# Forgetting loop with values of n-2, turns of n-1 and scores of n in one place; band and convolution with scores and values of neighbouring pairs together

## The chip, the cores and the metric

One core of a Trainium2 chip runs the whole program in one launch. The metric is the device time of an execution in microseconds (us): 1598.29 is the median of three runs of the kernel before, which lie between 1597.94 and 1598.76. The engines go by their names: TensorE (PE) multiplies, VectorE (DVE) and ScalarE (ACT) work element by element, GpSimd (POOL) and SyncE (SP) mostly start transfers. Each engine runs its own queue of instructions in order, and semaphores join the queues.

## The reference, cut

Two transformer blocks for 256 tokens with 1024 features, in float32. Three of their attention layers lie where the change is made:

```python
# first block, second layer: chunked ("band") attention, 12 heads of 64, beside 4 heads over a memory
s = jnp.einsum('bqhd,bkhd->bhqk', qc, kc) * scale + bias
p = jax.nn.softmax(jnp.where(valid, s, -jnp.inf), axis=-1)
o = jnp.einsum('bhqk,bkhd->bqhd', p, vc)
...
# second block, first layer: a convolution over 31 tokens with a layer norm and silu, beside
# sliding-window attention ("swa"), 8 heads of 64, 2 heads of keys and values
a = u * jax.nn.sigmoid(gate)
y = lax.conv_general_dilated(a, w, padding=[(CONV_K - 1, 0)], feature_group_count=CONV_CH) + b
yf = (y - mu) * lax.rsqrt(var + EPS) * ln_g + ln_b
...
# second block, second layer: forgetting attention ("fox"), 16 heads of 64
c = jnp.cumsum(log_sigmoid(zf + b_f))
sc = jnp.einsum("bhqd,bhkd->bhqk", qs, kh) / math.sqrt(dh) + cs[..., :, None] - c[..., None, :]
p = jax.nn.softmax(jnp.where(tpos >= key_pos, sc, NEG), axis=-1)
o = jnp.einsum("bhqk,bhkd->bhqd", p, vh)
return o.reshape(b, s, h * dh) @ w_out
```

Each layer ends in a product with w_out, and swiglu or convolutional feed-forward layers (FFN) stand between them.

## The kernel before

The order of every engine is written out by hand, one block for each: sync (from L571), gpsimd (L728), scalar (L856), vector (L1471) and tensor (L2213). No planner moves anything.

Weights stream through 520 slots of 128 x 1024 floats, in a ring of ten. SyncE loads a slot; `splits(t)` on ScalarE casts it to the high part w_hi (L870, 1 cast a slot); `splits(t)` on VectorE subtracts to get the low part w_lo (L1488). TensorE multiplies both with the activations, which are split in the same way, so a float32 product is three matmuls (`mm`, L2215 and L2216). Both engines work through the slots in order, and so each `splits` in their queues stands before all later work of that engine.

A projection of two heads (a part, `part(name, bank, i)`) has two halves i of 24 matmuls each and one slot each half; VectorE takes it out of its PSUM bank when both are done (`take_part`, L2007, and `take_pair` for the forgetting layer). An output chunk (`out_chunk`, called as `band_out(i, b)`, `swa_out(i, b)`, `fox_out(i, b)`) is six matmuls for features i and output half b.

Attention works on pairs of heads. A pair n goes through: `scores` on TensorE (L2462; L2456 is the decay row of the forgetting layer), `scores` on VectorE (masked sums with their maxima, L1696 and L1709), `exps` on ScalarE (L1059), `probs` on VectorE (reciprocal L1718 and the normalising product L1722), `turns` on TensorE (transposes, L2475), `pt_copy` on ScalarE (L1071), `values` on TensorE (L2485 and L2488), and `o_hi` on ScalarE (L1077) and `o_lo` on VectorE (L1728), which put the result by in two parts. All of a pair's PSUM lies in one of four places, handed out by WAYS (L223); `scores` waits until the pair that had the place before has been put by (`before[g]`). Probabilities alternate between two buffers.

In the forgetting layer TensorE (L2990 to L3027) runs over m = 1 to 3 with the parts of pair m, and between their halves come the scores of pairs 2m - 2 and 2m - 1, their turns and the values of the pair before. Pairs 6 and 7 come between output chunks. The loops of ScalarE (L1447 to L1464) and VectorE (L2187 to L2207) follow m in the same way. The slots of the parts are 430 + 4m + 2 part + i, the output's slots are 446 to 453, and the next FFN starts at 454. `splits(t + 8)` inside the loops belongs to a slot that TensorE reads four half parts later.

In the band layer (ScalarE from L1279, VectorE from L2009, TensorE from L2756) pairs 0 and 1 are those of the memory, and pairs 2 to 7 follow; projections of queries, keys and values (`band_part`, `project("VB", b)`) and output chunks lie between the steps. In the convolution layer (ScalarE from L1372, VectorE from L2087, TensorE from L2899) `stack`, `conv` and `turn_u` stand between the steps of four pairs. `conv(2)` and `conv(3)` read the turned u, which GpSimd's queue writes to DRAM and reads back stacked (L832 to L849). `mean` and `variance` belong to the layer norm.

The loop of the forgetting layer on TensorE, and those on the other two:

```python
for m in range(1, 4):                          # TensorE, L2990
    fox_part(m, 0, 0)
    if m > 1: values("fox", 2 * m - 3)
    fox_scores(2 * m - 2)
    fox_part(m, 0, 1)
    fox_scores(2 * m - 1)
    fox_part(m, 1, 0)
    turns("fox", 2 * m - 2)
    fox_part(m, 1, 1)
    ...
```

Of the kernel before, what the change touches and what calls it, by code (L numbers as in the profile page):

```python
# [14 lines left out]
NCH = D // P  # L15
SEQ = 256
NTB = SEQ // P
# [218 lines left out]
def build(nc, x, mem, norm_mix_g, norm_ffn_g, a_w_in, a_gate_b, a_conv_w, a_conv_b, a_head_g, a_w_out,  # L236
# [5 lines left out]
    with ctx:  # L242
# [614 lines left out]
        def _(act):  # L857
# [449 lines left out]
            exps("band", 4)  # L1307
            splits(133)
            pt_copy("band", 3)
            o_hi("band", 2)  # L1310
            splits(134)
            take_v("VB", 0, HALF, SEQ)
            pt_copy("band", 4)
            o_hi("band", 3)
# [11 lines left out]
            splits(139)  # L1326
            o_hi("band", 6)
            pt_copy("band", 7)
            splits(140)
            o_hi("band", 7)  # L1330
# [66 lines left out]
            take_gate(1, 1)  # L1397
            exps("swa", 3)
            take_turned_u(2)
            pt_copy("swa", 2)  # L1400
            splits(286)
            conv_out(0)
            splits(288)
            conv_out(1)
            o_hi("swa", 2)
            pt_copy("swa", 3)
            splits(289)
            o_hi("swa", 3)
# [38 lines left out]
            for m in range(4):  # L1447
                t = fox_slots(m, 0)
                splits(t + 8)
                if m == 3:  # L1450
                    o_hi("fox", 5)
                exps("fox", 2 * m)
                if m in (1, 2):
                    o_hi("fox", 2 * m - 1)
                splits(t + 9)
                exps("fox", 2 * m + 1)
                pt_copy("fox", 2 * m)
                splits(t + (11 if m == 3 else 10))
                pt_copy("fox", 2 * m + 1)
                o_hi("fox", 2 * m)  # L1460
# [11 lines left out]
        def _(dve):  # L1472
# [566 lines left out]
            splits(129)  # L2039
            take_part("K1", bank[4], qk[:, 8:10, :])  # L2040
            scores("band", 3)
            probs("band", 2)
            splits(131)
            scores("band", 4)
            probs("band", 3)
            splits(132)
            take_part("K2", bank[5], qk[:, 10:12, :])
            o_lo("band", 2)
            probs("band", 4)
            splits(134)  # L2050
            o_lo("band", 3)
# [10 lines left out]
            probs("band", 7)  # L2062
            o_lo("band", 6)
            splits(139)
# [47 lines left out]
            scores("swa", 3)  # L2112
            probs("swa", 2)
            splits(285)
            take_u(1, 1)
            take_turned_u(3)
# [70 lines left out]
            for m in range(4):  # L2187
                t = fox_slots(m, 0)
                if m:
                    o_lo("fox", 2 * m - 2)  # L2190
                splits(t + 8)
                scores("fox", 2 * m)
                if m:
                    o_lo("fox", 2 * m - 1)
                if m < 3:
                    take_pair(m + 1, 0)
                probs("fox", 2 * m)
                scores("fox", 2 * m + 1)
                splits(t + 9)
                probs("fox", 2 * m + 1)  # L2200
                splits(t + (11 if m == 3 else 10))
                if m < 3:
                    take_pair(m + 1, 1)
            o_lo("fox", 6)
            splits(454)
# [8 lines left out]
        def _(pe):  # L2214
# [565 lines left out]
            scores("band", 2)  # L2780
            values("band", 1)
            band_part("K1", bank[4], 1)
            scores("band", 3)
# [5 lines left out]
            turns("band", 3)  # L2789
            values("band", 2)  # L2790
            project("VB", 0)
            turns("band", 4)
            values("band", 3)
# [19 lines left out]
            values("band", 6)  # L2813
            turns("band", 7)
            band_out(3, 1)
            band_out(5, 0)
            band_out(4, 1)
            values("band", 7)
            band_out(6, 0)
            band_out(7, 0)  # L2820
            band_out(5, 1)
# [96 lines left out]
            project("GU1", 1, {3: [lambda: scores("swa", 3)]})  # L2918
# [6 lines left out]
            values("swa", 2)  # L2925
            turns("swa", 3)
            mean(0)
            mean(1)
            values("swa", 3)
            pe.wait_ge(u_taken[2], 1)  # L2930
            pe.wait_ge(u_taken[3], 1)
            swa_out(0, 1, 0)
# [119 lines left out]
```

## Time and profile before

| what | value |
|---|---|
| median of three runs | 1598.29 us |
| the profiled execution | 1599.74 us |
| its span in the trace | 1598.0 us |
| mean granted clock of TensorE, as a share of 2.4 GHz | 0.999 |
| TensorE busy with matmuls | 1587.4 us, 99% |
| its weight loads | 1354.9 us, 85% |
| VectorE busy | 1092.2 us, 68% |
| ScalarE busy | 919.5 us, 58% |
| GpSimd busy | 56.2 us, 4% |

Busy times are shares of the span. Matmuls are pipelined and the trace models their ends, so neighbouring ones overlap in the rows; start times are the recorded ones. In a timeline a row is a run of equal instructions: when it starts, how long it lasts, engine, line, operation, output and inputs, shapes and count; brackets at its end give the idle time of the engine before it and who ended that. The chain of waits follows the work that ended last back through whatever released it.

### The profile page before, as it was taken

Reading aid. Unit: us, or ns where it says so; the run is one execution under the profiler, and the core shown is the slowest. Engines: PE = TensorE matmul, PEld = TensorE weight load, DVE = VectorE, ACT = ScalarE, POOL = GpSimd, SP = SyncE. Lnnn points to the kernel's source line nnn. Section 1 sums busy time; section 2 is a strip of 40 time slices with the busy share of each in tenths; the row PEclk is TensorE's granted clock in tenths of the full one; section 3 lists DMA queues with packets and bytes.
Section 4 is the critical chain, followed back from the end, with each engine's and each line's share of the span. In section 5 each row is a group of like instructions: output and inputs, shape, how many; then the busy total and the mean of one; then the engine's idle time right before and its main releaser. Section 6 shows DMA issues by size and latency. Waiting matters only on the chain.

```text
span 1598.0 us, 23594 instructions
## 1 busy us (share of the span) xinstructions
PE 1587.4 (99%) x9256; PEld 1354.9 (85%) x9256; DVE 1092.2 (68%) x1759; ACT 919.5 (58%) x1555; POOL 56.2 (4%) x96
## 2 busy tenths in 40 slices
PE   9999999999999999999999999999999999999998
PEld 7898888889788888888887788888888889888887
DVE  5986867778677768656677466567565667775665
ACT  6766645567655546545476664447444484664544
POOL 4000000000030000000002100000000000000000
PEclk9999999999999999999999999999999999999999
DMA  8545675554355565566655555655666564356662
GB/s 299 146 146 189 217 238 192 186 174 144 118 193 190 175 199 179 188 197 189 191 159 161 143 191 186 196 185 171 210 185 188 181 200 146 119 184 199 184 189 75
DMA packets 212401, 287.67 MB, mean 180 GB/s; under 512 B 11100, under 2 KB 180382, under 8 KB 212292
## 3 DMA queue, kind: packets, MB, share of 16 engines
q1 hardware_dynamic: 208676, 280.00, 55.3%
q0 software_dynamic: 3616, 6.17, 1.4%
q8 instruction: 74, 1.21, 0.3%
q14 instruction: 35, 0.29, 0.1%
HBM read 284.47 MB, written 3.87 MB: 180 GB/s over the span
## 4 chain that ended last, share of the span: by engine, by line
PE 97%; DMA 1%; ACT 1%; issue 0%; SPq 0%; DVE 0%; POOL 0%; DVEq 0%; ACTq 0%
PE two L2216 91%; PE two L2293 1%; PE two L2462 1%; PE two L2475 1%; PE two L2485 1%; PE two L2870 0%; DMA vals<-u_dram 0%; PE two L2279 0%; PE two L2488 0%; DMA raw<-in_mem_w_kv 0%; PE two L2626 0%; DMA raw<-in_ffn_w_up 0%; DMA u_dram<-aux 0%; PE two L2456 0%; PE two L2844 0%
## 5 line engine op out<-in xcount | busy, mean ns | idle before, releaser
L2216 PE MATMUL two<-act_parts,w_hi 128*128 128x512 f32 (+1 forms) x2784 | 801.7, 353 | 0.0
L1488 DVE TENSOR_TENSOR w_lo<-raw,w_hi 128x1024 fp32r<-128x1024 f32 (+1 forms) x520 | 613.1, 1221 | 105.8 <-ACT w_hi L870 105.6
L2216 PE MATMUL two<-act_parts,w_lo 128*128 128x256 f32 x2256 | 635.0, 281 | 0.0
L2216 PEld LDWEIGHTS two<-act_parts,w_hi 128*128 128x128 f32 x2784 | 487.0, 188 | 81.1 <-issue 5.3
L870 ACT CAST w_hi<-raw 128x1024 fp32r<-128x1024 f32 (+1 forms) x522 | 516.6, 1046 | 5.5 <-DMA raw<-in_ffn_w_up 5.0
L2216 PEld LDWEIGHTS two<-act_parts,w_lo 128*128 128x128 f32 x2256 | 425.5, 189 | 2.1
L2216 PE MATMUL two<-w_hi,act_parts 128*128 128x512 f32 (+2 forms) x832 | 248.6, 378 | 1.5 <-ACT w_hi L870 1.2
L999 ACT COPY p_sb<-two 128x512 f32<-128x512 f32 x108 | 62.4, 578 | 247.1 <-PE two L2216 247.1
L2216 PE MATMUL two<-w_hi,hid_even 128*128 128x512 f32 x576 | 187.8, 393 | 0.0
L2216 PEld LDWEIGHTS two<-w_hi,act_parts 128*128 128x128 f32 x832 | 150.2, 188 | 33.4 <-issue 3.6
L1616 DVE TENSOR_TENSOR pt_sb<-two,p_sb 128x512 f32<-128x512 f32 x54 | 37.3, 691 | 198.4 <-ACT p_sb L999 198.4
L2216 PE MATMUL two<-w_hi,hid_odd 128*128 128x512 f32 x496 | 162.4, 394 | 0.0
L2216 PE MATMUL two<-w_lo,act_parts 128*128 128x512 f32 (+2 forms) x416 | 152.7, 372 | 0.0
L2216 PEld LDWEIGHTS two<-w_hi,hid_even 128*128 128x128 f32 x576 | 108.1, 188 | 25.3
L2216 PE MATMUL two<-w_lo,hid_even 128*128 128x512 f32 x288 | 113.5, 394 | 0.0
L2216 PEld LDWEIGHTS two<-w_hi,hid_odd 128*128 128x128 f32 x496 | 93.1, 188 | 22.1 <-issue 0.3
L2216 PE MATMUL two<-w_lo,hid_odd 128*128 128x512 f32 x248 | 97.7, 394 | 0.0
L2216 PEld LDWEIGHTS two<-w_lo,act_parts 128*128 128x128 f32 x416 | 78.1, 188 | 13.6 <-DVE w_lo L1488 0.4
L1020 ACT ACTIVATE p_sb<-pt_sb 128x512 f32<-128x512 f32 x60 | 38.0, 633 | 77.6 <-DVE pt_sb L1639 60.3
L920 ACT ACTIVATE act_parts<-two,par 128x128 fp32r<-128x128 f32 x160 | 44.5, 378 | 37.9 <-PE two L2293 37.8
L2216 PEld LDWEIGHTS two<-w_lo,hid_even 128*128 128x128 f32 x288 | 54.0, 188 | 11.5
L1505 DVE SCALAR_TENSOR_TENSOR act_parts<-two,par,act_parts 128x128 fp32r<-128x128 f32 x160 | 43.7, 343 | 24.2 <-ACT act_parts L920 24.2
(318 smaller groups left out, 1198.8 us busy)
## 6 DMA issues: line engine op xcount, KB each, us to landing
raw<-in_ffn_w_up SPq DMA_DIRECT2D x160, 512.0 KB, 3.9
raw<-in_ffn_w_down SPq DMA_DIRECT2D x132, 512.0 KB, 3.5
raw<-in_ffn_w_gate SPq DMA_DIRECT2D x80, 512.0 KB, 3.7
raw<-in_a_w_in SPq DMA_DIRECT2D x24, 512.0 KB, 4.3
raw<-in_fox_w_in SPq DMA_DIRECT2D x20, 512.0 KB, 3.8
raw<-in_ffn_w_up SPq DMA_DIRECT2D x32, 256.0 KB, 3.5
raw<-in_w_kv SPq DMA_DIRECT2D x12, 512.0 KB, 3.8
raw<-in_a_w_out SPq DMA_DIRECT2D x8, 512.0 KB, 3.8
```

Of the source, the lines that this page charges most:

```text
L870: nc.scalar.copy(w_hi[:, t % RING, k * n:(k + 1) * n], raw[:, t % RING, k * n:(k + 1) * n]).then_inc(hi_done, 1)
L920: nc.scalar.activation(act_part(0, c, b), x_turned(idx, b, c), ACT.Copy, scale=cols(col, c)).then_inc(ah, 1)
L999: nc.scalar.copy(half_sb[part], wide_half(part, 1)).then_inc(ff_half[part], 1)
L1020: nc.scalar.activation(gate_act, gate_cv_all if conv else gate_all, ACT.Silu).then_inc(ff_act, 1)
L1488: nc.vector.tensor_tensor(w_lo[:, r, 0:n], raw[:, r, 0:n], w_hi[:, r, 0:n], ALU.subtract).then_inc(lo_done, 1)
L1505: nc.vector.scalar_tensor_tensor(out=act_part(1, c, b), in0=x_turned(idx, b, c), scalar=cols(col, c), in1=act_part(0, c, b), op0=ALU.mult, ...
L1616: nc.vector.tensor_tensor(dst, wide_half(part, 0), half_sb[part], ALU.add).then_inc(ff_sum[part], 1)
L2216: return nc.tensor.matmul(dst, a, w, start=start, stop=stop, skip_group_check=True)
L2293: ins = nc.tensor.transpose(x_turned(idx, b, c), x_tok[:, b, c * P:(c + 1) * P], ident[:, :])
L2462: ins = nc.tensor.matmul(dst[half][:, lo:hi], q[:, b * P:(b + 1) * P], k[:, 0:hi - lo], start=kind != "fox", stop=True, skip_group_check=True)
L2475: ins = nc.tensor.transpose(place[g][:, half * 512 + dst:half * 512 + dst + P], p_sb[:, g % 2, half * 512 + src:half * 512 + src + P], ide ...
L2485: nc.tensor.matmul(place[g][DH * half:DH * (half + 1), 0:SEQ], head_v(kind, h0 + half, 0), pt_sb[:, g % 2, half * 512:half * 512 + SEQ], s ...
```

## The change

Only the order of calls changes, on three engines; no instruction is added or taken away, and nothing changes on SyncE's and GpSimd's queues.

- Forgetting layer: TensorE's loop has, after every second half part, one place where values of pair n - 2, turns of n - 1 and scores of n stand directly behind each other (`fox_stages(n)`). Before, scores 2m - 2 and 2m - 1 stood on either side of a half part and turns and values in places of their own. The last pairs follow the same pattern among the output chunks. ScalarE's loop becomes one over n with two casts, `o_hi(n - 2)`, `pt_copy(n - 1)` and `exps(n)` in each turn; VectorE's has two splits, `o_lo(n - 2)`, `scores(n)`, `take_pair` and `probs(n)`.
- Band layer: scores 3 go directly behind scores 2, values 2 in front of values 3 and behind the first half of the values' projection, values 6 directly in front of values 7. ScalarE's and VectorE's calls are moved to suit.
- Convolution layer: scores 3 come out of the gate and u projection and stand directly before the convolution; values 2 join values 3; output chunk (1, 0) goes ahead of conv(2); the chunks (1, 1) and (2, 0) stand around the variance. ScalarE copies turned probabilities 2 ahead of the turned u, VectorE takes scores 3 later.

The diff, with one line of context on either side of each place (`...` where lines are left out):

```diff
@@ -1305,13 +1305,13 @@
 exps("band", 4)
+pt_copy("band", 3)
 splits(133)
-pt_copy("band", 3)
-o_hi("band", 2)
 splits(134)
 take_v("VB", 0, HALF, SEQ)
+o_hi("band", 2)
+o_hi("band", 3)
 pt_copy("band", 4)
-o_hi("band", 3)
 splits(135)
@@ -1323,10 +1323,9 @@
 exps("band", 7)
-splits(139)
-o_hi("band", 6)
 pt_copy("band", 7)
 splits(140)
+o_hi("band", 6)
 o_hi("band", 7)
@@ -1395,17 +1394,18 @@
 take_gate(1, 1)
+pt_copy("swa", 2)
+take_turned_u(2)
 exps("swa", 3)
-take_turned_u(2)
-pt_copy("swa", 2)
 splits(286)
 conv_out(0)
+splits(287)
+conv_out(1)
+pt_copy("swa", 3)
 splits(288)
-conv_out(1)
 o_hi("swa", 2)
-pt_copy("swa", 3)
+o_hi("swa", 3)
 splits(289)
-o_hi("swa", 3)
 fetch_table(ACT.Sqrt)
@@ -1444,20 +1444,27 @@
 splits(435)
-for m in range(4):
-    t = fox_slots(m, 0)
+for n in range(6):
+    t = fox_slots(0, 0) + 2 * n
+    splits(t + 7)
+    if n >= 2:
+        o_hi("fox", n - 2)
+    if n >= 1:
+        pt_copy("fox", n - 1)
+    exps("fox", n)
     splits(t + 8)
-    if m == 3:
-        o_hi("fox", 5)
-    exps("fox", 2 * m)
-    if m in (1, 2):
-        o_hi("fox", 2 * m - 1)
-    splits(t + 9)
-    exps("fox", 2 * m + 1)
-    pt_copy("fox", 2 * m)
-    splits(t + (11 if m == 3 else 10))
-    pt_copy("fox", 2 * m + 1)
-    o_hi("fox", 2 * m)
+o_hi("fox", 4)
+pt_copy("fox", 5)
+splits(449)
+exps("fox", 6)
+splits(451)
+o_hi("fox", 5)
+pt_copy("fox", 6)
+splits(452)
+exps("fox", 7)
+splits(454)
+o_hi("fox", 6)
+pt_copy("fox", 7)
 splits(455)
@@ -2037,17 +2044,17 @@
 splits(129)
+probs("band", 2)
 take_part("K1", bank[4], qk[:, 8:10, :])
 scores("band", 3)
-probs("band", 2)
 splits(131)
+probs("band", 3)
 scores("band", 4)
-probs("band", 3)
 splits(132)
 take_part("K2", bank[5], qk[:, 10:12, :])
-o_lo("band", 2)
 probs("band", 4)
 splits(134)
+o_lo("band", 2)
 o_lo("band", 3)
@@ -2060,8 +2067,8 @@
 probs("band", 7)
+splits(139)
 o_lo("band", 6)
-splits(139)
 o_lo("band", 7)
@@ -2109,10 +2116,10 @@
 splits(284)
-scores("swa", 3)
 probs("swa", 2)
 splits(285)
 take_u(1, 1)
+scores("swa", 3)
 take_turned_u(3)
@@ -2184,25 +2191,27 @@
 take_pair(0, 1)
-for m in range(4):
-    t = fox_slots(m, 0)
-    if m:
-        o_lo("fox", 2 * m - 2)
+for n in range(6):
+    t = fox_slots(0, 0) + 2 * n
+    splits(t + 7)
+    if n >= 2:
+        o_lo("fox", n - 2)
+    scores("fox", n)
     splits(t + 8)
-    scores("fox", 2 * m)
-    if m:
-        o_lo("fox", 2 * m - 1)
-    if m < 3:
-        take_pair(m + 1, 0)
-    probs("fox", 2 * m)
-    scores("fox", 2 * m + 1)
-    splits(t + 9)
-    probs("fox", 2 * m + 1)
-    splits(t + (11 if m == 3 else 10))
-    if m < 3:
-        take_pair(m + 1, 1)
+    take_pair(n // 2 + 1, n % 2)
+    probs("fox", n)
+o_lo("fox", 4)
+scores("fox", 6)
+splits(450)
+probs("fox", 6)
+splits(451)
+o_lo("fox", 5)
+scores("fox", 7)
+splits(452)
+probs("fox", 7)
+splits(454)
 o_lo("fox", 6)
-splits(454)
+splits(455)
 o_lo("fox", 7)
@@ -2778,19 +2787,19 @@
 scores("band", 2)
+scores("band", 3)
 values("band", 1)
 band_part("K1", bank[4], 1)
-scores("band", 3)
 band_part("K2", bank[5], 0)
 turns("band", 2)
 pe.wait_ge(fp_taken, PI["K1"] + 1)
 scores("band", 4)
 band_part("K2", bank[5], 1)
 turns("band", 3)
+project("VB", 0)
 values("band", 2)
-project("VB", 0)
+values("band", 3)
 turns("band", 4)
-values("band", 3)
 pe.wait_ge(fp_taken, PI["K2"] + 1)
@@ -2810,15 +2819,15 @@
 band_out(2, 1)
-values("band", 6)
 turns("band", 7)
 band_out(3, 1)
 band_out(5, 0)
+values("band", 6)
+values("band", 7)
 band_out(4, 1)
-values("band", 7)
+band_out(5, 1)
 band_out(6, 0)
 band_out(7, 0)
-band_out(5, 1)
 out_end("band", band_ready, 1)
@@ -2915,33 +2924,36 @@
 stack(1)
-project("GU1", 1, {3: [lambda: scores("swa", 3)]})
+project("GU1", 1)
+scores("swa", 3)
 conv(0, 0, QUADS // 2)
 turns("swa", 2)
 turn_u(2)
 turn_u(3)
 conv(0, QUADS // 2)
 conv(1)
-values("swa", 2)
 turns("swa", 3)
 mean(0)
 mean(1)
+values("swa", 2)
 values("swa", 3)
 pe.wait_ge(u_taken[2], 1)
 pe.wait_ge(u_taken[3], 1)
 swa_out(0, 1, 0)
 pe.wait_ge(h_olo, PAIR0["swa"] + 4)
 swa_out(0, 0, 0)
+swa_out(1, 0)
 conv(2)
 conv(3)
 mean(2)
 mean(3)
+swa_out(1, 1)
+out_chunk("swa", swa_ready, 2, 0, (0,))
+variance()
+out_chunk("swa", swa_ready, 2, 0, (1,))
+swa_out(2, 1)
 for b in range(NTB):
-    swa_out(1, b)
-variance()
-for i in range(2, 4):
-    for b in range(NTB):
-        swa_out(i, b)
+    swa_out(3, b)
 for b in range(NTB):
@@ -2987,43 +2999,40 @@
 pe.wait_ge(gates_m, 2)
+def fox_stages(n):
+    if n >= 2:
+        values("fox", n - 2)
+    if n >= 1:
+        turns("fox", n - 1)
+    if n < 8:
+        fox_scores(n)
+
 for m in range(1, 4):
     fox_part(m, 0, 0)
-    if m > 1:
-        values("fox", 2 * m - 3)
-    fox_scores(2 * m - 2)
+    fox_stages(2 * m - 2)
     fox_part(m, 0, 1)
-    fox_scores(2 * m - 1)
     fox_part(m, 1, 0)
-    turns("fox", 2 * m - 2)
+    fox_stages(2 * m - 1)
     fox_part(m, 1, 1)
-    if m < 3:
-        turns("fox", 2 * m - 1)
-        values("fox", 2 * m - 2)
-values("fox", 4)
-turns("fox", 5)
 pe.wait_ge(h_olo, PAIR0["fox"] + 4)
 fox_out(0, 0)
+fox_stages(6)
 fox_out(1, 0)
-fox_scores(6)
-values("fox", 5)
 pe.wait_ge(h_olo, PAIR0["fox"] + 5)
 fox_out(0, 1)
 fox_out(1, 1)
-fox_scores(7)
-for b in range(NTB):
-    fox_out(2, b)
-turns("fox", 6)
-for b in range(NTB):
-    fox_out(3, b)
-turns("fox", 7)
-values("fox", 6)
+fox_out(2, 0)
+fox_stages(7)
+fox_out(2, 1)
+fox_out(3, 0)
+fox_out(3, 1)
 fox_out(4, 0)
+fox_stages(8)
+fox_out(4, 1)
 values("fox", 7)
 fox_out(5, 0)
 out_end("fox", pair_ready("fox", 0), 0)
-for i in range(4, NCH - 2):
-    fox_out(i, 1)
+fox_out(5, 1)
 out_end("fox", pair_ready("fox", 0), 1)
```

## Rows read from the trace of the kernel before

**Rows 1.** The page's fourth part: the chain that ended last, by engine.
```profile
PE 97%; DMA 1%; ACT 1%; issue 0%; SPq 0%; DVE 0%; POOL 0%; DVEq 0%; ACTq 0%
```

**Rows 2.** Windows: us, busy PE, PEld, DVE, ACT, POOL (instructions), clock, DMA share, GB/s.
```profile
1329.00:1405.00 76.00, 76.00 (x555) 64.23 (x554) 53.64 (x153) 45.81 (x110) 0.00 (x0) 1.00 0.40 122
880.00:893.00 13.00, 11.62 (x152) 7.06 (x151) 3.92 (x4) 5.73 (x9) 2.78 (x5) 1.00 0.65 128
```

**Rows 3.** Timeline, TensorE, forgetting stage: first row of each group of matmuls.
```profile
1347.18 0.50 PE L2216 MATMUL two<-act_parts,w_hi 128*128 128x256 f32 x2
...
1350.22 0.44 PE L2456 MATMUL two<-rowf,pick 64*128 64x384 f32 x2
...
1351.25 0.50 PE L2216 MATMUL two<-act_parts,w_hi 128*128 128x256 f32 x2
...
1354.21 0.82 PE L2475 MATMUL two<-ident,p_sb 128*128 128x128 f32 x6
1354.79 0.48 PE L2216 MATMUL two<-act_parts,w_hi 128*128 128x256 f32 x2
...
1357.72 0.82 PE L2475 MATMUL two<-ident,p_sb 128*128 128x128 f32 x6
1358.46 0.65 PE L2485 MATMUL two<-pt_sb,vals 128*64 128x256 f32 x4
...
1359.27 0.50 PE L2216 MATMUL two<-act_parts,w_hi 128*128 128x256 f32 x2
```

**Rows 4.** Timeline, TensorE, forgetting stage: turns that stand behind values.
```profile
1375.60 0.87 PE L2475 MATMUL two<-ident,p_sb 128*128 128x128 f32 x6
1376.23 0.48 PE L2216 MATMUL two<-w_hi,fox_parts 128*128 128x512 f32 x1
```

**Rows 5.** Chain of waits in order of time: start us, us, what.
```profile
398.17 0.76 PE two L2475 x6
398.93 0.86 PE two L2462 x8
...
402.83 0.80 PE two L2475 x6
...
843.62 1.51 PE two L2462 x16
...
1357.88 0.66 PE two L2475 x6
...
1388.82 2.79 PE two L2216 x12
```

**Rows 6.** Timeline, VectorE and ScalarE, softmax of a forgetting pair.
```profile
1347.31 0.29 DVE L1696 CUSTOM_DVE_ANT_0 aux<-two,causal 128x128 f32<-128x128 f32 x1 [1.17 <-PE two L2462]
...
1348.54 0.17 DVE L1709 TENSOR_SCALAR small<-small 128x4 f32<-128x4 f32 x1
...
1350.42 0.19 ACT L1059 ACTIVATION_READ_ACCUMULATOR p_sb<-aux,small 128x1 f32 x1
...
1350.77 1.05 ACT L870 CAST w_hi<-raw 128x1024 fp32r<-128x1024 f32 x1
...
1350.90 0.42 DVE L1728 TENSOR_TENSOR fox_parts<-two,fox_parts 128x256 fp32r<-128x256 f32 x1 [2.19 <-ACT fox_parts L1077]
1351.24 0.68 DVE L2007 TENSOR_TENSOR qk<-two,rstd 128x512 f32<-128x512 f32 x1
...
1352.05 1.01 DVE L1722 TENSOR_SCALAR p_sb<-p_sb,small 128x128 f32<-128x128 f32 x4
...
1354.28 1.22 DVE L1488 TENSOR_TENSOR w_lo<-raw,w_hi 128x1024 fp32r<-128x1024 f32 x1
```

**Rows 7.** Timeline, TensorE, band stage: values that waited.
```profile
390.12 0.65 PE L2485 MATMUL two<-pt_sb,mv 128*64 128x256 f32 x4 [0.25 <-ACT pt_sb L1071]
...
435.10 0.65 PE L2485 MATMUL two<-pt_sb,vals 128*64 128x256 f32 x4 [0.22 <-ACT pt_sb L1071]
```

**Rows 8.** Timeline, TensorE, convolution stage: conv(2) behind its reload.
```profile
885.73 0.42 PE L2870 MATMUL two<-qk,vals 128*32 128x256 f32 x3 [1.36 <-DMA vals<-u_dram]
```

## The prediction

> **What bounds the kernel now.** I read the chain of waits on the page first: TensorE holds 97% of the chain that ends last [rows 1]. Then I cut the span at the stages that the change edits. In the forgetting stage, 1329 to 1405 us, TensorE is busy for all 76.0 us, at a granted clock of 1.00, that is 2.4 GHz [rows 2]. So a microsecond that TensorE waits more, or works less, moves the end by as much, and what the other engines do counts only where TensorE waits for it. Then I read TensorE's start times, because the ends are modelled: the cost of a step is the distance from its start to the start of the next one.
>
> **What a border between groups costs.** A half part of a projection is 24 matmuls. Turns followed by a half part take 3.51 us from start to start (1354.21 to 1357.72), whatever stands on either side, which is 0.65 for six turns and 2.87 for the 24 [rows 3]. A half part between scores and scores takes 3.04 (1347.18 to 1350.22), between scores and turns 2.96 (1351.25 to 1354.21) [rows 3]. So leaving scores for a projection costs 0.10, entering scores from one costs 0.09, and turns cost nothing on either side. Turns followed by values take 0.74 instead of 0.65, so 0.09 again; values take 0.81 until the projection behind them starts [rows 3]. Values followed by turns: those turns take 0.63 to the next projection instead of 0.58 (1354.21 to 1354.79), so 0.05 [rows 3, 4]. Scores are 1.03 in this stage [rows 3]. A lone group of scores or values thus costs 0.19 at its borders, turns with one behind them 0.19, values with turns behind them 0.14.
> Two scores groups without anything between them take 1.51, one takes 0.86, so the second is 0.20 cheaper than the first [rows 5]. No row shows two values groups side by side; their saving lies between 0 and 0.20, and I take 0.15.
> The Trainium skill, TensorEngine Tiling (Array Packing), Key Properties, says that a change of tiling mode, though not of tile, drains TensorE. Counted by that rule alone, with turns as full-array work, the forgetting stage goes from 29 such changes to 32, which speaks against the change there; at about 0.2 us each it would add 0.6, twice what my rows give below.
>
> **Forgetting loop: borders.** Before there are five lone scores, three turns with values, two values with scores, one scores with values (0.19 each, 11 in all, 2.09), one values with turns (0.14) and one lone values (0.19): 2.42. After there are a lone scores, turns with scores, a lone values (0.19 each), a values with turns (0.14) and six places of values, turns, scores, at 0.09 + 0.05 + 0.09 + 0.10 = 0.33: 2.69. That is +0.3 us.
>
> **Forgetting loop: the softmax between scores(n) and turns(n).** This is the main term. VectorE starts 0.13 after TensorE has left the scores (1347.18, 1347.31) and ends its maxima at 1348.71, 1.40 later; the last sum of ScalarE's exponentials ends at 1350.61, 1.90 later [rows 6]. Taking the projection and normalising hold VectorE for 1.82, from 1351.24 to 1353.06, of which 0.60 are the taking and 1.22 the normalising [rows 6]. Alone, without cast and taking, that is 4.65, and with two hand-overs about 4.8 us. Before, the queues let it run nearly alone: the cast pair (ScalarE L870, VectorE L1488) that lies between scores and probs on VectorE has its ScalarE half ahead of the exponentials, and VectorE's half hides beside them.
> After, in each of the six turns of the loop, ScalarE has exps(n) and then splits(t + 8), while VectorE has scores(n), splits(t + 8), take_pair and then probs(n). VectorE must therefore wait for a cast that ScalarE starts only behind the exponentials. Queued behind that wait are take_pair, which empties the projection's bank, and probs(n), for which turns(n) on TensorE waits. The path becomes 0.13 + 1.40 + 1.90, the cast 0.96 (1.05, less the 0.09 by which neighbours overlap), a hand-over 0.04, L1488 1.14, L2007 0.60 (1.22 and 0.68, less 0.08 of overlap each), probs 1.22 and a hand-over 0.06: 7.45 us [rows 6].
> TensorE meanwhile has, from scores(n) to turns(n), two half parts and values(n-1): 2.96 + 2.87 + 0.09 + 0.81 = 6.73. So turns 1 to 4 wait 0.7 each. Turns 0 has no values before it, 5.83, and waits 1.6. Turns 5 has one half part, one output chunk (six matmuls; twelve take 2.79 [rows 5]) and values: 2.96 + 1.40 + 0.09 + 0.81 = 5.26, and waits 2.1. For turns 6 the path has no take_pair, 6.85, against four chunks and values, 0.10 + 5.58 + 0.09 + 0.81 = 6.58: 0.2. Scores 7 writes where pair 5 stood and waits for o_lo(5), which VectorE has behind probs(6) and one more split: 1.14 + 0.42 - 0.06 after turns 6 start, against 0.75 for the turns: 0.75. Turns 7 needs no cast behind its exponentials and has four chunks as cover. Sum: 1.6 + 2.8 + 2.1 + 0.2 + 0.75 = 7.45. Block 0's output still ends four chunks ahead of the normed turns, three of which cover its norm. Bounds: 0 if the casts cost nothing, 9 if each wait also makes the turns behind it start late, as in the band below.
>
> **Band.** Scores 3 moves up to scores 2, values 2 to values 3, values 6 to values 7. Borders before: scores 3 0.19, turns 2 with scores 4, turns 3 with values 2, turns 4 with values 3, 0.19 each; after: 0.19 for turns 2 with scores 4 and 0.14 for values 2, values 3, turns 4. Saved 0.76 - 0.33 = 0.43. At the end values with turns and a lone values, 0.33, become lone turns and one pair of values, 0.19: 0.14. Joining: 0.20 for scores, 0.15 twice for values. Waits: values 1 sat 0.25 behind the copy of its turned probabilities, values 7 sat 0.22 [rows 7]; scores 3 now stands ahead of the first, and the copy of the second now precedes the cast of a landing tile on ScalarE. Turns 2 and 3 take 0.76 and 0.80 from the release on instead of 0.66: they were nearly late, 0.24 together [rows 5]; probs 2 now goes ahead of take_part K1 and scores 3 on VectorE, which frees the first, and turns 3 keeps 0.3 of slack by the same durations. Sum 0.43 + 0.14 + 0.50 + 0.47 + 0.24 = 1.78; I take -1.8 us. Late hand-overs elsewhere (turns 7 lose the 0.95 of values 6 as cover) bound it at -1.2; -2.1 if every wait goes.
>
> **Convolution.** The scores that stood inside the GU1 projection join the convolution, values 2 join values 3: 0.19 + 0.15. But both lie ahead of conv(2), which waited 1.36 for its reload through DRAM [rows 8]; what they save ends in that wait. The gain is the output chunk (1, 0), 1.40, which moves from behind conv(3) into the wait. TensorE arrives 1.40 - 0.34 later, so 0.3 of the wait remains and the whole 1.40 is won, if the reload lands as before. ScalarE now copies turned probabilities (2) ahead of the u columns, where the exponentials stood: I allow 0.2. The variance now has nine matmuls ahead of it instead of twelve; 0.1 for that. So -1.1 us, between -0.5 and -1.4.
>
> **Sum.** 7.45 + 0.3 - 1.8 - 1.1 = +4.85 us. The profiled execution took 1599.74, with a span of 1598.0, and lies 1.45 above the median of the runs, 1598.29; the difference is made on the span, and its working carries over to the median: 1598.29 + 4.85 = 1603.1 us.
>
> **Rivals.**
> Half of the softmax path hides: the single waits of turns 1 to 4 and scores 7 vanish, because hand-overs are shorter than I put them or the casts slip ahead. This needs the path at 6.7 instead of 7.45. Then 1.6 + 2.1 + 0.3 - 2.9 = +1.1, 1599.4. Against it: the path is made of in-order queues with durations that repeat within 0.05. Chance 0.14.
> Faster: the softmax is wholly hidden and only borders and filled waits count. Mechanism: the cast for tile t + 8 is off the path, as in the kernel before, whose first pair takes 4.8. It decides below 5.26, the cover of turns 5. Then 0.3 - 2.9 = -2.6, 1595.7. Against it: ScalarE's order puts that cast behind the exponentials six times. Chance 0.06.
> Nothing gained in band and convolution, because other waits come up behind those removed: +7.75, 1606.0. For it: many hand-overs there are within 0.3. Chance 0.05.
> The clock falls while TensorE waits: in the loop one stretch of 8 us at 1.2 instead of 2.4 GHz would add about 8, 1611. Against it: over 880 to 893, with a wait of 1.36 in it, the granted clock is 1.00 [rows 2, 8], and the longest wait here is 2.1. Chance 0.03. The Trainium skill, TensorE: Matmul & The Clock Gate, Why this matters for your kernels, advises against idle gaps between bursts of matmuls because the clock falls back; the window of rows 2 does not show it for a wait of this size.
> The forecast keeps 0.72.
>
> **How the numbers follow.** About 0.2%, 3.2 us, is what a measurement of this kernel can tell from no change, so faster is below 1595.1 and slower above 1601.5. Forecast, nothing gained and the clock give slower, 0.80, less 0.03 of the forecast that may end below 1601.5: 0.77. Half hidden, that 0.03 and half of the faster rival, whose price is within 3.2: 0.20. Faster 0.03. The range goes from half hidden to just under the case without gains, 1599.8 to 1605.5, and leaves out some 0.16. Each unknown cost (values side by side, the reload, late starts at waits) lies inside it.
>
> **What the changed profile would show.** Turns (L2475) in the forgetting stage released by VectorE's L1722, 0.7 us each and two longer ones, with ScalarE's L870 straight behind the exponentials, then L1488 and L2007, then L1722. Band: no wait of values for L1071. Convolution: the wait for the reload down from 1.36 to some 0.3 to 0.5. I am wrong if the turns in the loop start without idle time, or if L1488 behind the scores starts before the exponentials end.

## The result and the profile after

The changed kernel took 1603.69 us, the median of six runs (1603.22 to 1604.42); the kernel before, run beside it, took 1598.51 (1597.94 to 1599.58). The ratio is 1.0033, with a 95% interval of 1.0020 to 1.0046: slower by 5.2 us, or between 3 and 7. Forecast were 4.85 us more, 1603.1, between 1599.8 and 1605.5. Three executions among the runs below took 1937 to 4467 us, one of the kernel with the cast moved and two of the kernel before, and all medians, ratios and intervals leave them out.

The page of the changed kernel, first its busy times, then the chain that ended last:

```profile
PE 1586.4 (99%) x9256; PEld 1355.0 (85%) x9256; DVE 1092.0 (68%) x1759; ACT 919.7 (57%) x1555; POOL 55.9 (3%) x96
...
PE 96%; DVE 2%; ACT 1%; issue 0%; DVEq 0%; POOL 0%; POOLq 0%; ACTq 0%
```

The numbers of instructions are those of before, and the busy times are within 1 us of them. In the chain VectorE had nothing [rows 1] and now has 2%. The forgetting stage, from the first scores to the first transposes of the next layer, lasted 75.98 us before (1329.20 to 1405.18) and lasts 83.93 after. The window of the stage after (columns as in [rows 2]) shows TensorE busy for 77.12 of these, where it was busy without a break before, at the same granted clock of 1.00, which is 2.4 GHz:

```profile
1324.73:1408.66 83.93, 77.12 (x554) 64.11 (x554) 53.30 (x153) 47.42 (x111) 0.00 (x0) 1.00 0.37 113
```

What TensorE waited for, over the whole span of the changed kernel (us in total, times, the longest):

```profile
PE two L2484 <- DVE p_sb L1729: 6.1, 7, 2.1
PE two L2567 <- POOL ident L734: 1.6, 1, 1.6
PE two L2225 <- ACT w_hi L870: 0.7, 2, 0.4
PE two L2465 <- DVE act_parts L1735: 0.7, 1, 0.7
PE two L2225 <- ACT act_parts L1103: 0.2, 1, 0.2
```

L2484 is the line of the turns (L2475 before), L1729 the last product of probs (L1722 before). The first line is new, and so is the fourth (scores 7 behind o_lo 5); the waits of the values for their copies [rows 7] and of the convolution for its reload [rows 8] are gone. One by one, from TensorE's timeline:

```profile
1333.16 0.87 PE L2484 MATMUL two<-ident,p_sb 128*128 128x128 f32 x6 [1.42 <-DVE p_sb L1729]
...
1342.40 0.87 PE L2484 MATMUL two<-ident,p_sb 128*128 128x128 f32 x6 [0.62 <-DVE p_sb L1729]
...
1351.64 0.87 PE L2484 MATMUL two<-ident,p_sb 128*128 128x128 f32 x6 [0.62 <-DVE p_sb L1729]
...
1370.11 0.87 PE L2484 MATMUL two<-ident,p_sb 128*128 128x128 f32 x6 [0.61 <-DVE p_sb L1729]
...
1379.36 0.88 PE L2484 MATMUL two<-ident,p_sb 128*128 128x128 f32 x6 [2.09 <-DVE p_sb L1729]
...
1388.01 0.88 PE L2484 MATMUL two<-ident,p_sb 128*128 128x128 f32 x6 [0.15 <-DVE p_sb L1729]
...
1389.56 0.44 PE L2465 MATMUL two<-rowf,pick 64*128 64x384 f32 x2 [0.68 <-DVE act_parts L1735]
```

These are turns 0, 1, 2, 4, 5 and 6, and scores 7; turns 3 wait 0.62 as well. Forecast were 1.6, four times 0.7, 2.1, 0.2 and 0.75. A wait costs more than its idle time in the row, which shows when the start times are laid beside those of a kernel with the same order on TensorE and almost no waits (split behind probs, below): turns 0 cost 1.64, because they also take 0.06 longer themselves, and the others about 0.07 more than their rows, 0.69 three times, 0.68, 2.16, 0.22 and 0.75. That is 7.52 us, against 7.45 of the forecast.

The chain of waits from scores 2 to turns 2 shows the way that this time goes:

```profile
1343.65 0.68 PE two L2471 x8
...
1345.59 0.18 DVE small L1716
1345.77 0.02 issue
1345.79 1.87 ACT p_sb L1059 x8
1347.66 0.95 ACT w_hi L870
1348.61 0.02 issue
1348.63 1.23 DVE w_lo L1495
1349.86 0.60 DVE qk L2014
...
1350.58 1.02 DVE p_sb L1729 x4
1351.60 0.04 issue
1351.64 0.87 PE two L2484 x6
```

Maxima, exponentials, then the cast of a weight slot, its split, the taking of the projection, and only then the normalising product. From the end of the scores, 1344.33, to the turns, 1351.64, that is 7.3 us; from the start of the projection behind the scores, 1344.23, it is 7.41. In the kernel before, the normalising product came ahead of the split whose cast stands behind the exponentials (1352.05 and 1354.28 in [rows 6]), so it did not wait for that cast.

All three stages lie between the same numbers of matmuls in every kernel of this study. Their lengths can therefore be compared by start times, counting TensorE's matmuls from 0: from the start of matmul 2250 to that of 2720 (band), from 4960 to 5400 (convolution) and from 7700 to 8300 (forgetting). The stretches between and behind them agree within 0.1 us in all traces; the one ahead of the band is 384.6 to 385.1 long. Lengths in us, the kernel before in four profiles:

| trace | band | convolution | forgetting |
|---|---|---|---|
| before, first profile | 73.07 | 52.93 | 85.35 |
| before, second profile | 73.59 | 52.71 | 85.35 |
| before, third profile | 74.03 | 52.24 | 85.35 |
| before, fourth profile | 73.29 | 51.74 | 85.35 |
| changed kernel | 70.81 | 51.16 | 93.29 |
| forgetting loop alone changed | 73.46 | 51.84 | 93.24 |
| band and convolution alone | 70.85 | 51.16 | 85.35 |
| band alone | 70.79 | 51.89 | 85.35 |
| convolution alone | 73.47 | 51.16 | 85.35 |
| split behind probs | 71.31 | 51.16 | 86.05 |
| cast ahead of exponentials | 71.71 | 51.14 | 86.73 |
| take_pair behind probs | 70.84 | 51.16 | 89.67 |
| pairs joined | 70.79 | 51.16 | 82.75 |

### The profile page after: what moved, and what is told of

Its sections match the earlier page's. It is cut to its first block, busy times and chain, and to the rows that moved or that the text cites. A ratio compares the mean times of both kernels' runs of the same rounds, so it can differ in the third digit from the quotient of the medians.

```text
span 1601.5 us, 23595 instructions
## 1 busy us (share of the span) xinstructions
PE 1586.4 (99%) x9256; PEld 1355.0 (85%) x9256; DVE 1092.0 (68%) x1759; ACT 919.7 (57%) x1555; POOL 55.9 (3%) x96
## 4 chain that ended last, share of the span: by engine, by line
PE 96%; DVE 2%; ACT 1%; issue 0%; DVEq 0%; POOL 0%; POOLq 0%; ACTq 0%
PE two L2225 89%; PE two L2302 1%; PE two L2471 1%; PE two L2484 1%; PE two L2879 1%; ACT p_sb L1059 1%; DVE w_lo L1495 1%; PE two L2494 1%; DVE aux L1703 1%; ACT w_hi L870 1%; DVE p_sb L1729 0%; PE two L2288 0%; PE two L2497 0%; PE two L2635 0%; DVE qk L2014 0%
```

## The experiments

### The forgetting loop alone

The diff is that of the change, without its places in the band and the convolution: on TensorE `fox_stages(n)` and the order of the output chunks, and ScalarE's and VectorE's loops over n.

> The forgetting loop of the changed kernel alone, band and convolution as before. Theory (the softmax of pair n now has a cast, a split and the taking of a projection in its queue): 7.45 us of waits and 0.3 of borders, +7.75 against the kernel before, 1606.2 if that is at 1598.5; turns in the stage wait for VectorE's L1722 by about 1.6, four times 0.7, 2.1 and 0.2. Rival (the loss of the whole change, measured at +5.2, is the loop's alone, and band and convolution gain nothing): +5.2, 1603.7. In the convolution the wait for the reload is that of the kernel before, 1.4; if it is near 0 here, the wait in the profile of before was a matter of that one execution.

Measured: 1607.98 us, 1.0054 of the kernel before (1.0041 to 1.0066), which ran at 1598.92 beside it. That is +9.1, between 6.6 and 10.6. The stage itself is 7.89 longer, with the waits of the changed kernel. So the loop loses more than the 5.2 that the rival gave it, and the rest of the change gives some of it back; that band and convolution gain nothing is out. The reload in the convolution, which this kernel does not touch, was waited for by 0.28, not 1.36.

### Band and convolution alone

The diff is the rest of the change.

> Band and convolution of the changed kernel, the forgetting loop as before. Prediction's terms: -1.8 and -1.1, together -2.9 against the kernel before. The two traces put the gain of the stages at -2.2 and -1.8, together -4.0. Rival (what these edits win is given back further on, or the reload waits elsewhere): 0.

Measured: 1595.68 us, 0.9979 (0.9971 to 0.9988), so -3.2 us, between -1.9 and -4.6. This is near the forecast of -2.9 and holds the -4.0 of the two traces as well; the rival's 0 is out. The forgetting stage is 85.35, to the hundredth that of before, so what was won upstream was kept.

### Convolution alone, band alone

```diff
-project("GU1", 1, {3: [lambda: scores("swa", 3)]})
+project("GU1", 1)
+scores("swa", 3)
...
 swa_out(0, 0, 0)
+swa_out(1, 0)
 conv(2)
```

```diff
 scores("band", 2)
+scores("band", 3)
 values("band", 1)
...
 values("band", 2)
+values("band", 3)
```

The first is TensorE's part of the convolution, the second that of the band, both cut to the core; ScalarE's and VectorE's moves of the change go with each.

> The convolution of the changed kernel alone, band and forgetting loop as before. Prediction's term: -1.1 against the kernel before (bounds -0.5 to -1.4), with 0.3 left of the wait for the reload. The two traces: -1.8, no wait left, because the write of the turned u landed sooner. Rival (the reload's landing varies from execution to execution, and the kernel before mostly waits less than the 1.36 of its profile): -0.5 or less.

Measured: 1598.30 us, 0.9994 (0.9985 to 1.0003): -0.6, anything from -2.4 to +0.5. That decides between none of the three values expected. In its profile the reload is not waited for, and the stage is 51.16 long.

> The band of the changed kernel alone, convolution and forgetting loop as before. Prediction's term: -1.8 against the kernel before (bounds -1.2 to -2.1); the stage in the traces says -2.2. The convolution is that of the kernel before, so its wait for the reload is looked at again: 1.36 in the profile of before, 0.3 in the one of the forgetting loop alone. If the wait varies by itself, a third value, anywhere from 0 to 1.4; if the forgetting loop had to do with it, 1.36.

Measured: 1596.28 us, 0.9985 (0.9976 to 0.9994), beside 1599.04 for the kernel before: -2.8 by the medians, between -1.0 and -3.8. Most of the gain is the band's, by the medians of the stages in the table 2.6 of 3.5. The convolution, left as before, waited 0.32 for its reload, so a third value did not appear, but neither did the 1.36.

### The kernel before, profiled three times more

> The kernel before, looked at again. The wait for the reload in the convolution was 1.36 in its first profile and 0.3 in the two experiments that leave the convolution as it was. If the landing varies by itself, this look and the next two lie between 0 and 1.4 and mostly near 0.3, and the convolution's term is then -1.77 + 1.36 - (the usual wait), about -0.7. If 1.36 belongs to this kernel, all three show 1.3 to 1.4. In the band, values 1 and 7 wait 0.2 to 0.6.

> As the look before this one: the wait for the reload mostly near 0.3 if its landing varies, 1.3 to 1.4 if it belongs to the kernel.

> As the two looks before this one: the wait for the reload mostly near 0.3 if its landing varies, 1.3 to 1.4 if it belongs to the kernel.

TensorE's timeline at conv(2), in the second profile and then in the fourth:

```profile
885.67 0.42 PE L2870 MATMUL two<-qk,vals 128*32 128x256 f32 x3 [1.14 <-DMA vals<-u_dram]
```

```profile
884.30 0.42 PE L2870 MATMUL two<-qk,vals 128*32 128x256 f32 x3 [0.17 <-DMA vals<-u_dram]
```

The third profile has 0.68. With the two experiments that leave this stage as it was, the waits are 0.17, 0.28, 0.32, 0.68, 1.14 and 1.36: the landing varies by itself, and the profile on which the prediction rests caught the longest of six. "Mostly near 0.3" did not come out: of the three new profiles only the fourth is near it, of all six traces three. GpSimd's queue shows where it comes from. The write of the turned u was issued at 873.21 in the first profile and 872.97 in the fourth, and the reload, which waits for that write, at 877.37 and 876.09: 4.16 and 3.12 later (first the first profile, then the fourth):

```profile
873.21 1.17 POOL L834 DMA_DIRECT2D u_dram<-aux  x2 [10.54 <-ACT aux L1361]
877.37 2.07 POOL L839 DMA_DIRECT2D qk<-u_dram  x3 [3.00 <-DMA u_dram<-aux]
```

```profile
872.97 1.17 POOL L834 DMA_DIRECT2D u_dram<-aux  x2 [10.54 <-ACT aux L1361]
876.09 2.07 POOL L839 DMA_DIRECT2D qk<-u_dram  x3 [1.95 <-DMA u_dram<-aux]
```

In the band, values 7 waited 0.22 in the first profile [rows 7], 0.76, 1.18 and 0.48 in the next three, 0.59 with the forgetting loop alone and 0.62 with the convolution alone; 0.2 to 0.6 had been expected. ScalarE of the third profile shows why (the next fence is TensorE of the same kernel):

```profile
433.50 1.05 ACT L870 CAST w_hi<-raw 128x1024 fp32r<-128x1024 f32 x1 [1.69 <-DMA raw<-in_ffn_w_up]
434.46 0.36 ACT L1077 CAST act_parts<-two 128x256 fp32r<-128x256 f32 x1
434.72 0.80 ACT L1071 COPY pt_sb<-two 128x768 f32<-128x768 f32 x1
```

```profile
435.58 0.65 PE L2485 MATMUL two<-pt_sb,vals 128*64 128x256 f32 x4 [1.18 <-ACT pt_sb L1071]
```

The copy of the turned probabilities stands behind a cast that waits for a weight slot to land. The change puts the copy ahead of that cast, and this wait is gone in every kernel that has the change's band. In two of their seven traces something else waits for the landing instead (cast ahead of the exponentials, below).

### The split moved behind probs

VectorE only, in the forgetting loop of the changed kernel:

```diff
     scores("fox", n)
-    splits(t + 8)
     take_pair(n // 2 + 1, n % 2)
     probs("fox", n)
+    splits(t + 8)
...
 scores("fox", 6)
-splits(450)
 probs("fox", 6)
-splits(451)
+splits(450)
 o_lo("fox", 5)
+splits(451)
```

> The changed kernel with VectorE's order in the forgetting loop alone altered: the split of the slot whose cast stands behind the exponentials goes behind probs(n) in all seven turns, and o_lo(5) goes ahead of one more split. TensorE's and ScalarE's orders stay. Theory: the path from scores to turns becomes 0.13 + 1.40 + 1.90 + 1.22 and two hand-overs, 4.8 us, less than the 5.26 to 6.73 that TensorE has in between, so all waits for L1722 go and the one for o_lo(5) falls to 0.3 or less: 7.0 to 7.4 us less than the changed kernel, about 4 us less than the kernel before counting by the traces' -4.0 for band and convolution and +0.3 for borders. Rival (values, turns and scores in one place cost by themselves, as three small groups between projections): the time stays near the changed kernel's, within 2 us, and TensorE's start-to-start times around the groups are longer by about a microsecond in each of six places.

Measured: 1596.60 us, 0.9984 (0.9975 to 0.9993). That is 7.1 us less than the changed kernel and about 2.3 less than the kernel before, where some 4 were expected: its band stage was half a microsecond longer than in the changed kernel (71.31, with a wait of 0.20 of the kind that the next section shows), and the convolution's usual gain is smaller than the traces had it. All waits for L1729 in the stage are gone; the one line left there is that of scores 7:

```profile
PE two L2465 <- DVE act_parts L1735: 0.2, 1, 0.2
```

VectorE now waits for the projection instead, while the exponentials run:

```profile
1352.75 0.17 DVE L1716 TENSOR_SCALAR small<-small 128x4 f32<-128x4 f32 x1
1354.55 0.69 DVE L2014 TENSOR_TENSOR qk<-two,rstd 128x512 f32<-128x512 f32 x1 [1.63 <-PE two L2225]
```

TensorE's order is the changed kernel's to the last instruction, so the three groups in one place are not what costs: the stage is 86.05, 0.70 above that of before. The wait of scores 7 is 0.29 of that from start to start, so the borders cost 0.4 and not 0.3.

### The cast moved ahead of the exponentials

ScalarE only, in the changed kernel:

```diff
     if n >= 1:
         pt_copy("fox", n - 1)
-    exps("fox", n)
     splits(t + 8)
+    exps("fox", n)
```

> The changed kernel with one thing altered, on ScalarE: in the six turns of the forgetting loop the cast of slot t + 8 goes ahead of the exponentials instead of behind them. VectorE still has the split of that slot and take_pair between scores(n) and probs(n). Theory (VectorE stands still because the cast comes late; its own 1.14 + 0.60 fit beside the 1.90 of the exponentials): path 0.13 + 1.40 + 1.90 + 1.22 and hand-overs, 4.8 us at the most 5.2, under the cover of 5.26 to 6.73; the waits of turns 0 to 5 go, 6.5 us in all, and turns 6 (0.2) and scores 7 (0.75) keep theirs: 6 to 6.5 less than the changed kernel. Rival (VectorE simply has too much between scores and probs, wherever the cast stands): the 1.74 stay on the path, 4.65 + 1.74 = 6.4, turns 0 still wait 0.6 and turns 5 1.1, and the gain is 4.8.

Measured: 1597.07 us, 0.9989 (0.9980 to 0.9998), 6.6 less than the changed kernel. In VectorE's timeline the split now starts at once behind the maxima and is over before the exponentials are, without leaving its place in the queue:

```profile
1344.09 0.17 DVE L1716 TENSOR_SCALAR small<-small 128x4 f32<-128x4 f32 x1
1344.17 1.22 DVE L1495 TENSOR_TENSOR w_lo<-raw,w_hi 128x1024 fp32r<-128x1024 f32 x1
1345.89 0.69 DVE L2014 TENSOR_TENSOR qk<-two,rstd 128x512 f32<-128x512 f32 x1 [0.51 <-PE two L2225]
```

The rival, by which VectorE has too much between scores and probs wherever the cast stands, asked for 4.8 and is out. It is the order of two queues against each other, not the amount of work, that made the wait. Scores 7 keep their 0.7 and turns 6 their 0.15; from start to start these are 0.98 of the 1.38 by which the stage is longer than before, and the borders the other 0.4.

Its band stage, which is that of the change, is 0.9 longer than in the changed kernel. The chain of waits there, up to an output chunk behind values 7:

```profile
427.25 6.53 DMA raw<-in_ffn_w_up
...
433.80 1.05 ACT w_hi L870
434.85 0.28 ACT act_parts L1077
...
435.15 0.44 DVE act_parts L1735
...
435.72 4.41 PE two L2225 x18
```

The cast waits for its weight slot as in the kernel before. Behind it stands no longer the copy but the putting by of values 6 and 7, and the chunk that reads them waits 0.67. In the kernel with the split moved the same chunk waits 0.20, in the five other traces with this band not at all. So the change gave the band more slack against the landing; it did not make it independent of it.

### take_pair moved behind probs

VectorE only, in the changed kernel:

```diff
     splits(t + 8)
-    take_pair(n // 2 + 1, n % 2)
     probs("fox", n)
+    take_pair(n // 2 + 1, n % 2)
```

> The changed kernel with one thing altered, on VectorE: in the six turns of the forgetting loop take_pair goes behind probs(n). The split of slot t + 8 stays ahead of probs, and its cast stays behind the exponentials. Theory: the path from scores to turns falls by the 0.60 of take_pair, from 7.45 to 6.85; turns 0 wait 1.0, turns 1 to 4 0.1 each, turns 5 1.6: 3.5 us less than the changed kernel. Rival (the path ends in the cast's hand-over, and take_pair is hidden beside something else): no change.

Measured: 1600.27 us, 1.0008 (0.9999 to 1.0017), 3.4 less than the changed kernel; the stage is 3.62 shorter (93.29 to 89.67). Turns 0 still wait 0.82 and turns 5 1.5; this is the waits view of that stretch of 1360 to 1385, where turns 5 stand:

```profile
PE two L2484 <- DVE p_sb L1729: 1.5, 1, 1.5
```

One 0.60 taken off the path shortens each of six waits by 0.60, which shows that take_pair is a link of the chain. Here turns 1 to 4 start 0.08 later than without a wait, too little to show as idle time in a row.

### Pairs joined

Band and convolution of the change, and a forgetting stage built from the border prices: TensorE's loop becomes

```python
for m in range(1, 4):
    fox_part(m, 0, 0)
    if m > 1:
        values("fox", 2 * m - 4)
        values("fox", 2 * m - 3)
    fox_scores(2 * m - 2)
    fox_scores(2 * m - 1)
    fox_part(m, 0, 1)
    fox_part(m, 1, 0)
    turns("fox", 2 * m - 2)
    fox_part(m, 1, 1)
    turns("fox", 2 * m - 1)
```

and VectorE's order in it is split, o_lo twice, scores twice, split, probs, take_pair, split, probs, split, take_pair; ScalarE does a cast ahead of both exponentials.

> Band and convolution of the changed kernel, and a new forgetting stage: for each m one place with values 2m - 4, values 2m - 3, scores 2m - 2, scores 2m - 1, turns alone between half parts or chunks, the same for pairs 6 and 7; on VectorE one split between scores and probs, whose cast stands ahead of the exponentials. By the border prices of the prediction: five places at 0.19, less four joinings of scores at 0.20 and four of values at 0.15, -0.45, against 2.42 in the kernel before: 2.9 less than with band and convolution alone (1595.7), 1592.8. What speaks against: scores 2m - 1 go where pair 2m - 4 stood, whose o_lo must be done within the 1.48 that values 2m - 3 and scores 2m - 2 take; if it is late, up to 0.5 in each of three places is lost, and the gain is 1.5 or less. Rival (small groups cost the same wherever they stand): no gain against 1595.7.

Measured: 1593.17 us (1592.76 to 1593.58), 0.9964 (0.9951 to 0.9977) of the kernel before: faster than both, by 5.9 and 10.5 us. The stage is 2.60 shorter than before, of 2.87 expected, and no row of TensorE in it shows a wait. One place of four groups, in TensorE's timeline:

```profile
1339.88 0.65 PE L2486 MATMUL two<-pt_sb,vals 128*64 128x256 f32 x4
1340.36 0.39 PE L2489 MATMUL two<-pt_sb,vals 128*64 128x128 f32 x4
1340.58 0.60 PE L2486 MATMUL two<-pt_sb,vals 128*64 128x256 f32 x4
1341.01 0.39 PE L2489 MATMUL two<-pt_sb,vals 128*64 128x128 f32 x4
1341.33 0.45 PE L2457 MATMUL two<-rowf,pick 64*128 64x384 f32 x2
1341.62 0.82 PE L2463 MATMUL two<-qk 64*128 64x128 f32 x8
1342.08 0.53 PE L2457 MATMUL two<-rowf,pick 64*128 64x384 f32 x2
1342.45 0.82 PE L2463 MATMUL two<-qk 64*128 64x128 f32 x8
1343.20 0.50 PE L2217 MATMUL two<-act_parts,w_hi 128*128 128x256 f32 x2
```

Values with values behind them take 0.70 (1339.88 to 1340.58), the second 0.75; two scores take 1.87 (1341.33 to 1343.20) instead of twice 1.03 [rows 3]. The joining of scores saves 0.19 here. That of values saves 0.15, as the prediction took it: the two take 1.45 (1339.88 to 1341.33) instead of twice the 0.80 that values take in the kernel before (1345.36 to 1346.16). The 0.27 that are missing lie in the place of pairs 4 to 7. There the two scores take 2.12 instead of 1.87, and the second starts at 1373.47, 0.15 behind the end of VectorE's o_lo(5), whose place in PSUM it takes:

```profile
1372.90 0.42 DVE L1729 TENSOR_TENSOR act_parts<-two,act_parts 128x256 fp32r<-128x256 f32 x1 [0.23 <-ACT act_parts L1077]
```

That fits the late hand-over which the expectation named, at half the price and in one place of three. The modelled ends of the matmuls fill the gap, so only start times show it.

## Why the prediction was right, and where its terms were off

The forecast's main term held step by step. The path from scores(n) to turns(n) was put at 7.45 us and is 7.41; the cover was put at 6.73 and is 6.72 (7.41 less the wait of 0.69, and the same from 1342.85 to 1349.57 in the kernel with the split moved); the waits were put at 7.45 and come to 7.52. That this is the cause and not something beside it is shown by two kernels that move calls on one engine alone and take the waits away (6.6 and 7.1 us), and by one that takes 0.60 out of the path and gets 3.4 back.

The borders of the forgetting loop were put at +0.3. The stage is 7.94 longer, of which 7.52 are waits; the remaining 0.4 agrees with the 0.4 of the two kernels with the split or the cast moved. So this term was too small by 0.1. The Trainium skill, TensorEngine Tiling (Array Packing), Key Properties, has TensorE drain at a change of tiling mode; counted by that alone, at 0.2 a change, the prediction had 0.6. No row gave those 0.2; the prediction's rows have 0.19 for the two borders of a lone group. The runs lie between the 0.6 and the sum of the rows. The three changes more (32 instead of 29) cost 0.14 each by the start times, and the kernel with pairs joined, which has 13, is 2.85 shorter without its late hand-over, 0.18 for each of 16 changes fewer. So the count points the right way in both, and 0.2 was a little too dear.

The convolution's term, -1.1, came near with errors that go against each other. It took the wait of 1.36 in one profile [rows 8] as the kernel's own, where the median of six traces is 0.5. On the other side, the 0.2 allowed for the exponentials, the 0.1 for the variance and the 0.3 that was to remain of the wait did not show in any trace. Without its wait the stage is 51.56 or 51.57 long in all six traces, and in the changed kernel 51.16: the gain is 0.41, for which the prediction had 0.34, and whatever the wait would have been. By the medians (52.07 and 51.16) that is 0.9, and against the one profile 1.77. By the prediction's working TensorE comes to the reload 1.06 later than before (1.40 less 0.34), and the two longest of the six waits exceed that. That no trace with the change waits goes together with something else: the reload is issued 2.55 to 3.14 behind the write in these seven traces, and 3.12 to 4.16 behind it in the six without. Whether the change brings that about is not shown.

The band's term, -1.8, was too small. By the medians of the stage, 73.47 before and 70.84 after, the band gains 2.6 us, beyond the bound of 2.1. Some 0.4 of the difference is again one execution taken for the kernel: the wait of 0.22 for values 7 [rows 7] is the shortest of six, with a median of 0.6. Against the profile that was read the band gains 2.26, still 0.5 more than forecast. Of that, 0.14 is a step missed in the working: a wait costs some 0.07 more than its idle time in the row. Another 0.23 is an output chunk that comes late in every trace of the old band, and in none of the changed one but the two with the wait shown above. In the first profile its first weight load stands idle 0.40 behind VectorE, at 437.52; the matmul before that takes 0.39 to the next start and the one behind it 0.31, where those around take 0.23. The rest of 0.1 is open.

Band and convolution together are 3.2 by the runs and 3.5 by the medians of their stages, for 2.9 forecast. The sum of stages is 7.9 - 2.6 - 0.9 = +4.4, the runs say +5.2 with an interval that holds it. The forecast of +4.85 lies between the two, but so near a hit is finer than the interval and partly luck: the band won 0.8 more than its term, the other three terms came out 0.1 to 0.2 worse. A wait for a transfer, read from one execution, was the weak place of this prediction, in both terms.

Of the rivals, the clock did not fall: the stage with waits of up to 2.09 has a granted clock of 1.00. The Trainium skill, TensorE: Matmul & The Clock Gate, Why this matters for your kernels, advises against idle gaps; for gaps of this size no run here shows a fall. The softmax was not half hidden, and the faster rival's condition, a cast off the path, is just what the kernels with the cast or the split moved made true; they came out at 1596.6 and 1597.1, for which the prediction had given 1595.7.

What stays open is why the reload can follow the write of the turned u after 3.1 us at one time and 4.2 at another, and after less in the kernels with the change. The weights that stream in at the same time are a candidate; no run here varied them.

## What to carry to other kernels

When a softmax moves to another place in the order, follow each instruction that its engines have queued between its steps, above all one that waits for a third engine: here one cast behind the exponentials put itself, its split and the taking of a projection on the path, and moving one call took 6.6 us away. What is joined on TensorE pays only while the other engines' path stays shorter than the work in between, so work out both before choosing the place. Before a wait for a transfer carries a term of a sum, look at several executions; one profile gave 1.36 where the others gave 0.2 to 1.1.

## What the runs showed of the hardware that was not expected

The same kernel's forgetting stage, which waits for no transfer, lasted 85.35 us in all seven traces that have it, while the band stage as before lay between 73.07 and 74.03 and the convolution between 51.74 and 52.93, and both follow the one wait behind a transfer that each holds: with 0.22, 0.48, 0.59, 0.62, 0.76 and 1.18 for values 7 the band took 73.07, 73.29, 73.46, 73.47, 73.59 and 74.03, and with 0.17, 0.28, 0.32, 0.68, 1.14 and 1.36 for the reload the convolution took 51.74, 51.84, 51.89, 52.24, 52.71 and 52.93. With both waits gone the runs draw together: eleven runs of band and convolution changed lie between 1595.41 and 1596.26, the 27 of the kernel before beside them between 1597.89 and 1600.29. Eleven of the kernel with the split moved, whose profile has the wait of 0.20 in the band, lie between 1596.05 and 1597.47.

A second group of scores straight behind the first saved 0.19 to 0.20 us in the forgetting stage too. Values take as long to scores behind them as to a projection: 0.80 in the kernel before (1345.36 to 1346.16) where a projection starts after 0.81 [rows 3], and 0.75 where they stand behind other values, to scores (1340.58 to 1341.33) as to a projection (1387.91 to 1388.66).
